# A two-block network in one program: the opening with modulation products on column strips, norms in four steps, and two weight panels multiplied inside the norm loop

## The chip, the cores and the metric

The kernel runs on one core of a Trainium2 chip, as one program. The metric is the device time of one execution in microseconds (us). The change is small against the whole, so the text works in single microseconds.

## What is computed

Two blocks follow each other on 512 tokens of width 1024. The first is a hybrid layer with 256 context tokens beside the 512; the second (attention, a delta rule and two gated feed-forward networks) isn't touched. The part around the change is the head of the hybrid layer:

```
mod   = silu(c) @ ada_w + ada_b                      # 6 * 1024 columns
mod_c = silu(c_ctx) @ ada_w + ada_b
sh1, sc1, g1, sh2, sc2, g2 = split(mod, 6)           # the same for mod_c
h  = rms_norm(x,   norm1_w) * (1 + sc1)  + sh1       # 512 tokens
hc = rms_norm(ctx, norm1_w) * (1 + sc1c) + sh1c      # 256 tokens
p  = h @ w_in                                        # q, k, v, z, xbc, dt
```

All products are in fp32 to the eye of the reference. The kernel makes a large product from three: operand and weights are each split in a high and a low part of type fp32r.

## The kernel before

**Layout.** Features lie on the partitions, in 8 chunks of 128, and tokens along the free dimension. `hh` and `hl` hold the high and the low part of the normed input: for each chunk 512 columns of x and 256 of the context.

**One plan for all engines.** `put` appends a step to a single list. At the end each engine walks through that list and issues, in that order, what the step means for it. So each engine's order is fixed when the program is built, and a step that waits on an engine holds all later steps on that engine. A semaphore wait on TensorE therefore also holds the products of other steps behind it. SyncE issues the loads, in the same order.

**Panels.** A weight panel is 1024 x 128 (512 KB). `load` brings it to one of three buffers `raw0` to `raw2` in turn, `cut` makes its high part on ScalarE (L612) and its low part on VectorE or GpSimd (L622), and `product` multiplies it, chunk by chunk, three products a chunk (high by high, high by low, low by high; L644). Two pairs of split buffers take turns: panel j+2 can be cut only when panel j's products are done. The panels come in the order q (4, on x alone), k and v (4 each, on x and context), dt, xbc, z and so on. Between panels the stream of loads also carries 32 parts of the modulation (`mod`) that are needed late: GpSimd makes them from a panel of `ada_w`, and TensorE and VectorE finish them (`modset`).

**The opening.** `turn_x` turns x and the context to the feature layout: TensorE transposes, ScalarE squares with a sum (L795) and copies (L800). `roots` and `spread` make the reciprocal root of the mean square and spread it over the partitions (L527, L488, L540). Then 16 panels of `ada_w` give scale and shift of the 8 chunks, two panels for each chunk. For panel i, `ada_mm` multiplies (L768) with the two columns silu(c), silu(c_ctx) as weights, 8 products that accumulate in two rows; ScalarE copies the two rows out (L813); `ada_set` transposes them (L776) and VectorE adds the bias (L831). After each second panel `norm1` handles one chunk: VectorE makes the gain (L836) and the scaled x (L846), ScalarE the high part (L819), VectorE the low part (L850), and the same three for the context. All 16 panels and 8 chunks come ahead of the first cut. The load of the second weight panel waits for the last `ada_set`, since `raw2` holds the copied rows until then.

```
for i in range(16):
    if i < 15:
        put("ada_mm", i + 1, banks=1, of=8)
    put("ada_set", i, banks=1, of=8)
    if i % 2:
        put("norm1", i // 2)
```

**A loop that exists already.** `gemm` has a form with `feed`, used later in the program: it calls `feed(c)`, puts the products of the first panel with chunk c, and then those of the second panel with chunk c - 2 (`LAG` is 2), and the third panel is cut after the last chunk.

## Time and profile before

| what | value |
|---|---|
| median of three runs | 2761.59 us (2761.25 to 2764.94) |
| the profiled execution | 2769.39 us, its span 2767.6 us |
| mean granted TensorE clock in it | 0.962 |
| TensorE busy | 2574.6 us, 93% of the span |
| VectorE, ScalarE, GpSimd busy | 50%, 35%, 36% |
| mean DMA rate | 73 GB/s |

The profiled execution has its own time, some 8 us over the median. Differences worked out from its rows are carried over to the median. Starts are in us from the beginning of the span. Neighbouring instructions of one engine overlap in the trace by some tens of nanoseconds, so costs are read from start to start where that can be done. An fp32 product or transpose shows as two records, an fp32r product as one. "PEclk" is the granted clock of TensorE: 1.00 is 2.4 GHz and 0.50 is 1.2 GHz.

### The profile page before, as it was taken

The numbers are of one execution on the slowest core, as the hardware profiler recorded it, in microseconds if no ns is written. First come the engines' busy times: TensorE is split into PE (matmuls) and PEld (weight loads), VectorE is DVE, ScalarE is ACT, GpSimd is POOL, SyncE is SP. The second block draws the span as 40 slices with busy tenths as digits, with TensorE's granted clock in tenths as the row PEclk, the third lists the DMA queues.
The fourth block names the chain that finished last, engine by engine and source line by source line (L and its number), as shares of the span: only waits on it lengthen the run. The fifth ranks groups of instructions, "written<-read, shape, count | busy, mean of one in ns | idle before, by whom it ended". The sixth has DMA issues, their size and how long they took to land.

```text
span 2767.6 us, 45664 instructions
## 1 busy us (share of the span) xinstructions
PE 2574.6 (93%) x19756; PEld 2307.6 (83%) x19756; DVE 1382.0 (50%) x2118; ACT 969.6 (35%) x1525; POOL 986.8 (36%) x585
## 2 busy tenths in 40 slices
PE   6999977899999999999999999999999989999997
PEld 4777766768888787887989999988988978999997
DVE  3545548363535354444175364466654534726363
ACT  4233442332323443333343332354333233333232
POOL 0653334634444422222534444500002214444444
PEclk8999988999999999999999999999998998999998
DMA  7532220323333221111222333322111012233321
GB/s 197 140 110 63 61 78 1 100 75 92 97 93 89 72 62 33 52 39 47 69 62 84 92 89 87 85 66 62 40 40 32 21 32 58 79 90 88 89 86 60
DMA packets 379929, 201.34 MB, mean 73 GB/s; under 512 B 6465, under 2 KB 377153, under 8 KB 379729
## 3 DMA queue, kind: packets, MB, share of 16 engines
q1 hardware_dynamic: 379728, 198.42, 25.5%
q8 instruction: 156, 2.56, 0.4%
q14 instruction: 45, 0.36, 0.0%
HBM read 196.30 MB, written 2.10 MB: 72 GB/s over the span
## 4 chain that ended last, share of the span: by engine, by line
PE 58%; DVE 22%; ACT 10%; issue 5%; POOL 3%; DMA 1%; SPq 0%; POOLq 0%; ACTq 0%; DVEq 0%
PE ps L644 41%; DVE t_ffy L2781 7%; ACT t_wh L612 4%; DVE t_ffy L2784 2%; ACT t_ffy L2688 2%; DVE t_atq L2580 2%; POOL t_wl L622 1%; PE ps L2388 1%; DVE t_ffy L2790 1%; PE ps L3013 1%; DVE t_wl L622 1%; PE ps L2361 1%; PE ps L2327 1%; PE ps L3032 1%; PE ps L1042 1%
## 5 line engine op out<-in xcount | busy, mean ns | idle before, releaser
L622 POOL TENSOR_TENSOR t_wl<-t_raw,t_wh 128x1024 fp32r<-128x1024 f32 (+2 forms) x268 | 610.9, 2280 | 1035.0 <-ACT t_wh L612 1035.0
L612 ACT ACTIVATE t_wh<-t_raw 128x1024 fp32r<-128x1024 f32 (+2 forms) x323 | 327.8, 1015 | 602.4 <-PE ps L644 571.6
L644 PE MATMUL ps<-t_hh,t_wh 128*128 128x264 f32 (+2 forms) x2048 | 474.0, 310 | 15.9 <-ACT t_wh L612 7.7
L644 PE MATMUL ps<-t_hh,t_wl 128*128 128x264 f32 (+2 forms) x2048 | 450.4, 299 | 5.9 <-POOL t_wl L622 5.3
L644 PE MATMUL ps<-t_hl,t_wh 128*128 128x264 f32 (+2 forms) x2048 | 447.5, 300 | 0.0
L644 PEld LDWEIGHTS ps<-t_hh,t_wh 128*128 128x128 f32 x2048 | 324.9, 193 | 38.0 <-issue 16.6
L644 PEld LDWEIGHTS ps<-t_hh,t_wl 128*128 128x128 f32 x2048 | 325.7, 192 | 21.1 <-POOL t_wl L622 6.3
L644 PEld LDWEIGHTS ps<-t_hl,t_wh 128*128 128x128 f32 x2048 | 324.1, 192 | 9.4 <-issue 1.5
L644 PE MATMUL ps<-t_fhh,t_wh 128*128 128x264 f32 (+1 forms) x1040 | 281.9, 325 | 7.6 <-DVE t_fhl L1705 5.6
L644 PE MATMUL ps<-t_fhh,t_wl 128*128 128x264 f32 (+1 forms) x1040 | 280.6, 324 | 4.3 <-POOL t_wl L622 4.2
L2781 DVE SCALAR_TENSOR_TENSOR t_ffy<-t_ffp,t_vec,t_ffy 128x528 f32<-128x528 f32 x88 | 216.4, 2459 | 130.6 <-ACT t_ffy L2688 130.6
L644 PE MATMUL ps<-t_fhl,t_wh 128*128 128x264 f32 (+1 forms) x1040 | 278.3, 323 | 0.0
L644 PEld LDWEIGHTS ps<-t_fhh,t_wh 128*128 128x128 f32 x1040 | 173.8, 190 | 26.8 <-DVE t_fhl L1705 8.2
L644 PEld LDWEIGHTS ps<-t_fhh,t_wl 128*128 128x128 f32 x1040 | 174.1, 190 | 21.6 <-POOL t_wl L622 5.6
L644 PEld LDWEIGHTS ps<-t_fhl,t_wh 128*128 128x128 f32 x1040 | 173.7, 189 | 16.7 <-issue 0.4
L644 PE MATMUL ps<-t_ffh,t_wl 128*128 128x264 f32 x704 | 144.8, 287 | 8.7 <-POOL t_wl L622 7.8
L644 PE MATMUL ps<-t_ffh,t_wh 128*128 128x264 f32 x704 | 144.7, 287 | 5.3 <-ACT t_wh L612 1.5
L644 PE MATMUL ps<-t_ffl,t_wh 128*128 128x264 f32 x704 | 143.4, 285 | 0.0
L2514 DVE TENSOR_TENSOR t_ffp<-ps,t_rstd 128x264 f32<-128x264 f32 x176 | 67.4, 424 | 112.8 <-PE ps L644 111.5
L622 DVE TENSOR_TENSOR t_wl<-t_raw,t_wh 128x1024 fp32r<-128x1024 f32 x55 | 78.4, 1427 | 84.6 <-ACT t_wh L612 84.6
L644 PEld LDWEIGHTS ps<-t_ffh,t_wl 128*128 128x128 f32 x704 | 109.5, 189 | 12.0 <-POOL t_wl L622 12.0
L644 PEld LDWEIGHTS ps<-t_ffh,t_wh 128*128 128x128 f32 x704 | 109.2, 190 | 6.9 <-ACT t_wh L612 5.0
(555 smaller groups left out, 4407.6 us busy)
## 6 DMA issues: line engine op xcount, KB each, us to landing
t_raw<-in_up SPq DMA_DIRECT2D x44, 512.0 KB, 3.9
t_raw<-in_up2a SPq DMA_DIRECT2D x44, 512.0 KB, 3.9
t_raw<-in_up2b SPq DMA_DIRECT2D x44, 512.0 KB, 3.8
t_raw<-in_attn_in SPq DMA_DIRECT2D x33, 512.0 KB, 4.1
t_raw<-in_dn_in SPq DMA_DIRECT2D x33, 512.0 KB, 4.2
t_raw<-in_ada_w SPq DMA_DIRECT2D x32, 512.0 KB, 4.6
t_raw<-in_w_in SPq DMA_DIRECT2D x25, 512.0 KB, 4.2
t_raw<-in_down SPq DMA_DIRECT2D x16, 512.0 KB, 3.8
```

The costliest lines, as they stand in the source:

```text
L612: ac.activation(wh[slot_of[j]][:, 0:kc, :], raw[r % NRAW][:, 0:kc, :], ACT.Copy).then_inc(up("wh_cut", "cut", j), 1)
L622: eng.tensor_tensor(wl[slot_of[j]][:, 0:kc, :], raw[r % NRAW][:, 0:kc, :], wh[slot_of[j]][:, 0:kc, :].bitcast(F), SUB).then_inc(up(name, " ...
L644: ins = pe.matmul(ps[bank_of(j, i)][:, 0:tn], wt[slot][:, k, :], a[:, k, t0:t0 + tn], start=first, stop=last)
L1042: ins = pe.matmul(ps[b][:, 0:64], pts[i % 2][:, 128 * k:128 * k + 128], V[:, v, 64 * h:64 * h + 64], start=k == 0, stop=k == 3)
L2327: pe.matmul(ps[b][0:tn, 0:wide], aq[p % 3][64 * e:64 * e + 64, t0:t0 + tn], ak[p % 3][64 * e:64 * e + 64, a:a + wide], start=True, stop=False)
L2361: pe.matmul(ps[b][0:tn, 0:wide], ak[p % 3][64 * e:64 * e + 64, t0:t0 + tn], aq[p % 3][64 * e:64 * e + 64, q0:q0 + wide], start=True, stop= ...
L2388: ins = pe.matmul(ps[b][64 * e:64 * e + 64, lo - q0:lo - q0 + n], lhs, pT[e][0:tn, P_AT[k] + lo - t0:P_AT[k] + lo - t0 + n], start=k == 0, ...
L2514: ins = dv.tensor_tensor(a[part_, t0:t0 + tn], ap[part_, :], rstd[part_, t0:t0 + tn], MUL)
L2580: dv.reciprocal(tq[m][:, :], tq[m][:, :]).then_inc(up("inverted", "pair_norm", p, m), 1)
L2688: ac.activation(y, fp[par][:, 0:L], ACT.Copy, scale=col(f"f{n}c0", f + NF * par)).then_inc(up("copied", kind, n, f), 1)
L2781: dv.scalar_tensor_tensor(out=y, in0=u[:, 1:1 + L], scalar=col(f"f{n}c1", f + NF * par), in1=y, op0=MUL, op1=ADD).then_inc(st.up(), 1)
L2784: dv.scalar_tensor_tensor(out=y, in0=u[:, 2:2 + L], scalar=col(f"f{n}c2", f + NF * par), in1=y, op0=MUL, op1=ADD).then_inc(up("conved", ki ...
```

## The change

1. `ada_mm` puts its 8 products on four column strips of 32 (k modulo 4 picks the strip); its weights are 32 columns wide (`cs32`, two of them filled, the others zero), and its result has 128 rows. `ada_set` becomes a product of these 128 rows with `add4`, which adds the four strips and turns in one.
2. `norm1` is taken apart into four steps a chunk: scaled x, scaled context (`norm1`), low x, low context (`low1`). The low part of the context of chunk c is put into the turn of chunk c + 1.
3. The products of q's first two panels go into the norm loop: `gemm` gets `feed_first`. In the turn of chunk c come two `ada_mm` and two `ada_set` of the next chunk, the norm steps of c, panel 0 with chunk c, and panel 1 with chunk c - 2.
4. Loads 0 and 1 are now both weight panels and are issued straight behind the first three panels of `ada_w`, and the cuts of both come before the loop. The other `ada_w` loads follow in `ada_rest`. The `mod` parts start with the third panel, and dt gets two.
5. `silu_c` moves to the front; both `roots`, `ada_mm` 0 and 1 and `ada_set` 0 are put ahead of the `spread` steps; the table load for `rope` is put into the first turn.

```diff
--- before.py
+++ after.py
@@ -195,9 +195,10 @@
...
-                if ada_at and stage in ("q", "k", "v", "dt", "xbc", "z", "wo"):
-                    stream.append(("mod", 32 - len(ada_at)))
-                    ada_at.pop(0)
+                for _ in range(2 if stage == "dt" else 1):
+                    if ada_at and len(panels) > 2 and stage in ("q", "k", "v", "dt", "xbc", "z", "wo"):
+                        stream.append(("mod", 32 - len(ada_at)))
+                        ada_at.pop(0)
...
@@ -685,7 +686,10 @@
...
-        row2 = [rows_of(raw[2])[0:2, 128 * i:128 * i + 128] for i in range(2)]
+        spare = rows_of(raw[2])
+        rows2 = [spare[:, 128 * i:128 * i + 128] for i in range(2)]
+        cs32 = spare[:, 256:512].rearrange("p (c j) -> p c j", j=32)
+        add4 = spare[:, 512:514]
...
+            "begin": "scaled/z scaled/s", "norm1": "normed hi_set", "low1": "lo_dve",
...
         put("begin")
+        put("silu_c")
         for i in range(7):
             put("turn_x", i, banks=2, of=8)
             if i < 6:
                 sig.mark("squared", "turn_x", i)
-        put("silu_c")
+        load_to(1)
+        put("ada_rest")
         put_roots(NORM_X)
+        put_roots(NORM_C)
+        put("ada_mm", 0, banks=1)
+        put("ada_mm", 1, banks=1)
+        put("ada_set", 0, banks=1)
         put_spread(NORM_X)
-        put_roots(NORM_C)
         put_spread(NORM_C)
-        put("ada_mm", 0, banks=1, of=8)
-        for i in range(16):
-            if i < 15:
-                put("ada_mm", i + 1, banks=1, of=8)
-            put("ada_set", i, banks=1, of=8)
-            if i % 2:
-                put("norm1", i // 2)
-                take_sqb(("lo_dve", "norm1", i // 2, "x"), "norm1", i // 2, "x")
-                take_sqb(("lo_dve", "norm1", i // 2, "c"), "norm1", i // 2, "c")
+
+        def norm1_of(c, x):
+            put("norm1", c, x)
+            take_sqb(("lo_dve", "low1", c, x), "norm1", c, x)
+
+        def feed_first(c):
+            if c is None:
+                return
+            if c == 0:
+                put("rope_tables")
+            if c < KD:
+                for i in (2 * c + 2, 2 * c + 3):
+                    if i < 16:
+                        put("ada_mm", i, banks=1)
+                    put("ada_set", i - 1, banks=1)
+                    if i == 16:
+                        break
+                norm1_of(c, "x")
+            if 0 < c <= KD:
+                put("low1", c - 1, "c")
+            if c < KD:
+                norm1_of(c, "c")
+                put("low1", c, "x")
 
         def ready_h(p, k):
-            return [("lo_dve", "norm1", k, "c" if len(p.spans) == 2 else "x")]
+            return [("lo_dve", "low1", k, x) for x in "xc"[:len(p.spans)]]
...
-                for i in range(7):
+                for i in range(3):
                     ada_panel(i)
...
-            def turn_x(i):
-                w.wait_ge(s.copied, at("copied", "turn_x", i, "1"))
-                ada_panel(7 + i)
+            def ada_rest():
+                for i in range(3, 7):
+                    ada_panel(i)
+                for i in range(7):
+                    w.wait_ge(s.copied, at("copied", "turn_x", i, "1"))
+                    ada_panel(7 + i)
...
-                    ins = pe.matmul(ps[b][0:2, 0:128], cs[:, k, :], x[:, k, :], start=k == 0, stop=k == KD - 1)
+                    ins = pe.matmul(ps[b][32 * (k % 4):32 * (k % 4) + 32, 0:128], cs32[:, k, :], x[:, k, :], start=k < 4,
+                                    stop=k >= 4)
...
-                pe.transpose(ps[b][:, 0:2], row2[i % 2], C("ident", 2, 2)).then_inc(up("turned", "ada_set", i), 1)
+                w.wait_ge(s.scaled, at("scaled", "begin", "s"))
+                pe.matmul(ps[b][:, 0:2], rows2[i % 2], add4, start=True,
+                          stop=True).then_inc(up("turned", "ada_set", i), 1)
...
+                w.wait_ge(s.scaled, at("scaled", "begin", "z"))
+                ac.activation(cs32[:, :, 0], col("c", 0, 8), ACT.Silu)
+                ac.activation(cs32[:, :, 1], col("c_ctx", 0, 8), ACT.Silu).then_inc(up("cs_ready", "silu_c"), 1)
...
-                ac.activation(row2[i % 2], ps[b][0:2, 0:128], ACT.Copy).then_inc(up("copied", "ada_mm", i), 1)
-
-            def norm1(c):
-                for x, a in (("x", (0, S, 0)), ("c", (S, S + CT, 1))):
...
+                ac.activation(rows2[i % 2], ps[b][:, 0:128], ACT.Copy).then_inc(up("copied", "ada_mm", i), 1)
+
+            def norm1(c, x):
+                a, n, g = (0, S, 0) if x == "x" else (S, CT, 1)
+                i, _ = sqb_at["norm1", c, x]
+                w.wait_ge(s.normed, at("normed", "norm1", c, x))
...
             def begin():
                 dv.memset(eps[:, :], EPS).then_inc(s.eps_set, 1)
+                dv.memset(cs32[:, :, :], 0.0).then_inc(up("scaled", "begin", "z"), 1)
+                w.wait_ge(s.cst_in, 16)
+                dv.tensor_reduce(add4, C("ident").rearrange("p (g h) -> p h g", h=32)[:, 0:2, :], AX.X,
+                                 ADD).then_inc(up("scaled", "begin", "s"), 1)
...
-            def norm1(c):
-                w.wait_ge(s.mod_set, at("mod_set", "ada_set", 2 * c + 1))
-                dv.tensor_scalar(gain1[:, 0:2, c], mod[:, SC1 + c, :], 1.0, col("norm1_w", c), ADD,
...
+            def norm1(c, x):
+                a, n, g, src = (0, S, 0, xl[c]) if x == "x" else (S, CT, 1, ctxT[:, c, :])
+                i, last = sqb_at["norm1", c, x]
+                if x == "x":
+                    w.wait_ge(s.mod_set, at("mod_set", "ada_set", 2 * c + 1))
+                    dv.tensor_scalar(gain1[:, 0:2, c], mod[:, SC1 + c, :], 1.0, col("norm1_w", c), ADD,
+                                     MUL).then_inc(st.up(), 1)
...
+                w.wait_ge(s.rstd_a, at("rstd_a", "spread", NORM_X if x == "x" else NORM_C))
+                if last:
+                    w.wait_ge(handles[last[0]], at(*last))
+                dv.scalar_tensor_tensor(out=sqb[i][:, 0:n], in0=src, scalar=gain1[:, g, c:c + 1], in1=rstd[:, a:a + n],
+                                        op0=MUL, op1=MUL).then_inc(up("normed", "norm1", c, x), 1)
...
+            def low1(c, x):
+                a, n, g = (0, S, 0) if x == "x" else (S, CT, 1)
+                i, _ = sqb_at["norm1", c, x]
+                w.wait_ge(s.hi_set, at("hi_set", "norm1", c, x))
+                dv.scalar_tensor_tensor(out=hl[:, c, a:a + n], in0=sqb[i][:, 0:n], scalar=mod[:, c, g:g + 1],
+                                        in1=hh[:, c, a:a + n].bitcast(F), op0=ADD,
+                                        op1=SUB).then_inc(up("lo_dve", "low1", c, x), 1)
...
-        load_to(NRAW - 1)
-        put("rope_tables")
-        gemm(("q",), then_first)
+        gemm(("q",), then_first, feed=feed_first)
```

## Rows read from the trace of the kernel before

**Rows 1.** The page, part 1: busy time and share of the span by engine.
```profile
PE 2574.6 (93%) x19756; PEld 2307.6 (83%) x19756; DVE 1382.0 (50%) x2118; ACT 969.6 (35%) x1525; POOL 986.8 (36%) x585
```

**Rows 2.** Windows: stretch, length, busy us (count) by engine, PEclk, DMA share, GB/s.
```profile
20.00:33.00 13.00, 8.01 (x37) 5.66 (x38) 0.34 (x2) 5.02 (x12) 0.00 (x0) 0.52 1.19 290
33.00:53.00 20.00, 18.97 (x162) 13.19 (x159) 12.16 (x25) 5.74 (x15) 4.73 (x4) 1.00 0.77 189
...
70.00:74.00 4.00, 0.00 (x0) 0.00 (x0) 2.45 (x5) 1.90 (x3) 0.00 (x0) 0.50 0.84 258
74.00:80.00 6.00, 5.63 (x12) 3.97 (x13) 2.36 (x2) 1.33 (x2) 0.27 (x1) 0.50 0.59 163
```

**Rows 3.** Timeline of the first chunk: start, us, engine, line, what [idle before].
```profile
35.85 0.22 PE L776 MATMUL ps<-t_cst,t_raw 2*128 2x2 f32 x1
...
36.11 0.22 DVE L831 TENSOR_SCALAR t_mod<-ps,t_vec 128x2 f32<-128x2 f32 x1 [1.77 <-PE ps L776]
36.36 0.23 DVE L836 TENSOR_SCALAR t_gain<-t_mod,t_vec 128x2 f32<-128x2 f32 x1
36.62 0.75 DVE L846 SCALAR_TENSOR_TENSOR t_sqb<-t_xT,t_gain,t_rstd 128x512 f32<-128x512 f32 x1
...
37.41 0.72 ACT L819 ACTIVATE t_hh<-t_sqb,t_mod 128x512 fp32r<-128x512 f32 x1 [1.19 <-DVE t_sqb L846]
...
38.17 0.75 DVE L850 SCALAR_TENSOR_TENSOR t_hl<-t_sqb,t_mod,t_hh 128x512 fp32r<-128x512 f32 x1 [0.79 <-ACT t_hh L819]
```

**Rows 4.** Timeline, TensorE: cuts of the first panels and the first products.
```profile
73.24 2.15 ACT L612 ACTIVATE t_wh<-t_raw 128x1024 fp32r<-128x1024 f32 x2
...
74.31 2.36 DVE L622 TENSOR_TENSOR t_wl<-t_raw,t_wh 128x1024 fp32r<-128x1024 f32 x2 [0.46 <-ACT t_wh L612]
...
74.33 0.79 PE L644 MATMUL ps<-t_hh,t_wh 128*128 128x512 f32 x1 [4.87 <-ACT t_wh L612]
...
74.92 0.63 PE L644 MATMUL ps<-t_hl,t_wh 128*128 128x512 f32 x1
...
88.31 0.39 PE L644 MATMUL ps<-t_hh,t_wh 128*128 128x512 f32 x1
88.54 0.39 PE L644 MATMUL ps<-t_hl,t_wh 128*128 128x512 f32 x1
```

**Rows 5.** Timeline of the opening: ScalarE's tables and roots, TensorE's spreads.
```profile
20.44 1.28 ACT L805 ACT_TABLE_LOAD   x1
...
23.36 0.30 ACT L527 ACTIVATE t_roots<-t_ssq,t_eps 128x4 f32<-128x4 f32 x1
...
23.92 2.07 PE L488 MATMUL ps<-t_cst,t_roots 128*128 128x128 f32 x8 [7.79 <-DVE t_roots L560]
```

**Rows 6.** Timeline, TensorE: two panels of the modulation, at either clock.
```profile
28.21 3.57 PE L768 MATMUL ps<-t_vT,t_small 128*2 128x128 f32 x16
...
34.01 1.91 PE L768 MATMUL ps<-t_xbc,t_small 128*2 128x128 f32 x16
```

**Rows 7.** Timeline, TensorE: a sum on column strips (L2724), later in the program.
```profile
948.50 0.42 PE L2724 MATMUL ps<-t_atq,t_cst 128*32 128x264 f32 x2
...
949.21 0.39 PE L2724 MATMUL ps<-t_sqb,t_cst 128*32 128x264 f32 x2
...
949.53 0.39 PE L644 MATMUL ps<-t_hh,t_wh 128*128 128x264 f32 x1
```

**Rows 8.** Timeline, TensorE: one fp32 product with 128 weight columns among others.
```profile
166.56 0.28 PE L783 MATMUL ps<-t_cst,t_part 128*128 128x1 f32 x2
```

**Rows 9.** Windows, TensorE alone: short pauses between bursts, in the scan stage.
```profile
443.00:446.00 3.00, 1.03 (x12) 1.00 0.00 0
...
457.00:459.00 2.00, 0.15 (x2) 1.00 0.00 0
459.00:463.00 4.00, 4.00 (x33) 0.57 0.01 4
```

**Rows 10.** The page, part 6: loads of weight panels: count, size, us to landing.
```profile
t_raw<-in_w_in SPq DMA_DIRECT2D x25, 512.0 KB, 4.2
```

More of the change, by code:

```diff
@@ L745, in ada_mm @@
                     ada_panel(14 + i)
-            return {"begin": begin, "turn_x": turn_x, "ada_mm": ada_mm}
+            return {"begin": begin, "ada_rest": ada_rest, "ada_mm": ada_mm}
         def front_tensor(pe, w, held, free):
@@ L858, in modset @@
                                  ADD).then_inc(up("mod_set", "modset", n), 1)
-            return {"begin": begin, "ada_set": ada_set, "norm1": norm1, "modset": modset}
+            return {"begin": begin, "ada_set": ada_set, "norm1": norm1, "low1": low1, "modset": modset}
         def front_gpsimd(po, w, st):
```

26 lines of the change are left out of this document (4 added, 22 removed).

## The prediction

> **What bounds the kernel now.** I read the page first: TensorE is busy for 93% of the span [rows 1], so over most of the program only TensorE's work and its waits count. The windows show where that doesn't hold, and the reader is to see that the change sits there: TensorE idles four microseconds just before the first product at 74.33, and the clock is at its lower level then and for six microseconds of products after it [rows 2]. The timeline of one chunk shows what the opening waits on: a chain of VectorE and ScalarE steps that pass one tile to and fro [rows 3]. TensorE is nearly full beside it from 33 to 53, but with the small products of the modulation [rows 2, 6]. The DMA engines run at 290 GB/s to 33 and at 189 in the mean of 33 to 53 [rows 2]; 3.8 MB at 290 take 13 us, so they are dry from about 46, and the loads don't set the pace there. From 80 on TensorE is full. What the change is worth is therefore the start of panel q2, the first product that neither version mixes into the norms: 88.31 before, since q0 and q1 take from 74.33 up to there [rows 4]. Any shift of it is carried to the end, because the order behind it is unchanged and TensorE-bound.
>
> **What the change removes and moves.** Removed: 16 panels of `ada_mm` at 1.91 us each at the full clock or 3.57 at the lower [rows 6], and the stretch 74.33 to 88.31 as a stretch of its own. Added: strips, a wider `ada_set`, and above all a new order on TensorE. The product of q0 with chunk c waits for the low part of x of that chunk, and in TensorE's list the `ada_mm` and `ada_set` that VectorE needs for chunk c+1 stand behind it. VectorE's next step in turn waits for them. So the loop becomes a ring: products, modulation, norm chain, products, with little of it beside anything else. Before, the norm chain and the modulation ran side by side.
>
> **When the loop begins.** ScalarE's copies end at 20.44. One table load goes (silu is done early, while ScalarE waits for x), so the first root starts at 21.7, two roots of 0.3 us end at 22.3, then two copies of rows (0.27 each). TensorE does `ada_set` 0 (0.5 at the lower clock) and both spreads, 2.07 us and half as much, together 3.1 [rows 5], and ends at 26.1. ScalarE's copy of the context's root ends at 26.5, the two cuts take 2.15 [rows 4] to 28.6. VectorE's two low parts take 2.36 [rows 4] to 30.0. Then bias and gain, scaled x, high and low part as in [rows 3]: from bias start to the end of the low part 36.11 to 38.92, and a second bias: the low part of chunk 0 is done at 33.0. Panels of `ada_w`, 512 KB each, come at 290 GB/s [rows 2], 1.8 us each, behind the two weight panels: the fourth by about 25 and the last by about 46, ahead of each turn. The lower bound here is 31 (cuts beside the spreads' end), the upper 35 (weight panels late); I take 33.
>
> **One turn of the ring**, from the low part of chunk c to that of c+1. First number the full clock, second the lower:
> - q0 with chunk c, three products of 512 columns: 0.23 each at the full clock (88.31 to 88.54), 0.43 at the lower, the first after a wait 0.59 (74.33 to 74.92) [rows 4]: 0.80, 1.45.
> - q1 with chunk c-2: 0.68, 1.28.
> - two `ada_mm`. No row has this form. The nearest is the sum on four strips: 16 records of 264 columns from 948.50 to the next product at 949.53, so 1.03 us; with 128 columns 0.48 to 0.50, and at the lower clock 0.9 [rows 7]. The other bound is no gain from strips, 1.91 and 3.57 [rows 6]. I take the strips, since they are the same form in the same program: 0.96, 1.80.
> - the first `ada_set`, now two records with 128 weight columns, 0.28 by [rows 8]: 0.25, 0.40.
> - four changes between whole array and strips: the last strip record starts at 949.21 and the next product at 949.53, where 0.22 is a strip's pace: 0.1 each [rows 7]: 0.40, 0.45.
> - the second `ada_set` until VectorE starts, 0.26 before for two weight rows [rows 3], with wide weights 0.35, 0.55.
> - bias 0.25, gain 0.26, scaled x 0.79, high part 0.76, low part 0.80 [rows 3]: 2.86 at either clock. The context's steps hide in the wait for ScalarE; uncovered they would cost about 0.8, half of x's two VectorE steps, the context being half as wide.
>
> That is 6.30 or 8.79 us. Two of the seven turns lack q1 (5.62, 7.51), the last lacks the `ada_mm` (4.89, 6.36). Sum: 41.3 or 56.5. Behind it stand q0's last chunk and three of q1: 2.8 or 5.3. q2 needs its load, which waits for the last `ada_set` and takes 4.2 us [rows 10], then a cut of 1.06: that is 5.3 after `ada_set` 15, while q1 ends 6 to 9 us after it, so q1 hides it; without that cover it would cost up to 1 us. The load of q3 and of the first `mod` part, and the rope tables, are queued behind that load on SyncE; with 1.5 MB at 290 GB/s they land about 5 us later, under q2. Two `mod` parts at dt are 9.5 us of GpSimd (4.73 for one, the four instructions of 33 to 53 [rows 2]) beside dt and two panels of 24 products each on 768 columns, at 0.34 us (0.23 for 512) 8 us a panel, so they cost nothing; if one of the next loads waited for them, it would be up to 1 us.
>
> The Trainium skill (TensorEngine Tiling, Key Properties) says that a change of the tiling mode drains TensorE, which speaks against switching four times a turn; the rows of the strips agree, with 0.1 us a change. Without that rule the sum would be some 2.5 us less. The skill (TensorE: Matmul & The Clock Gate, Part 3) gives a measured 2.38 times for three column strips; by that a block would take 0.80 at the full clock and the twelve blocks of the turns 4 us more.
>
> **The clock decides.** q2 starts at 33.0 + 41.3 + 2.8 = 77.1 if the clock is full all through, at 33.0 + 56.5 + 5.3 = 94.8 if it is low. In between it is 77.1 + 17.7 s for a share s at the lower level; 88.31 is met at s = 0.63. Each turn leaves TensorE idle for 3.2 us. In the scan stage a pause of 2 us brings the lower level for over three microseconds in one place (457 to 463) and not in another (443 to 446) [rows 9], and in the opening six microseconds of products passed before the level rose [rows 2]. The loop also starts at the lower level, after the idle time at 17 to 33. A burst at the lower level is 5.5 us long, so the clock should rise near its end, when the pause comes. I take s = 0.8: 77.1 + 14.2 = 91.3. That is 3.0 us later than before. From the median: 2761.6 + 3.0 = 2764.6 us. (The span of the profiled execution would go from 2767.6 to 2770.6; its own time is 8 us above the median, and the difference is carried over.)
>
> **The rivals.**
> - *The clock stays at its full level.* Bursts and pauses are as dense as in the stretch at 443 that kept it [rows 9]. Against it: the pause here is longer than 2 us in every turn, and the loop starts low. q2 at 77.1, 11.2 us early: 2750.4, faster. It decides from s below 0.32, where the gain passes 5.5 us.
> - *The clock stays low throughout.* The bursts hold strips and small products, and q2's first products would still be slow. q2 at 94.8 and up to 1 us for the rise: 2768 to 2769, slower. It decides from s above 0.94, or from 0.4 us more a turn than I count.
> - *The strips don't run side by side.* Fourteen blocks stay at 3.57 in place of 0.9, 2.7 us each: 37 us, so about 2800. The rows of the strips speak against it [rows 7].
> - *The ring isn't closed*, because VectorE's or ScalarE's steps overlap more than I see, or the changes and the wide `ada_set` are hidden: up to 1 us a turn less, 2757.
>
> **How the numbers follow.** A measurement of this kernel tells about 0.2%, or 5.5 us, from no change. I give the forecast (s about 0.6 to 0.94) 0.48, the full clock or most of it 0.22, the low clock throughout or longer turns 0.24, the open ring 0.05 (half of it inside 5.5 us), serial strips 0.01. So faster 0.27, same 0.48, slower 0.25. The time is that of the likeliest, 2764.6; its own range is 2759 to 2768. The range for 8 times in 10 takes in the full clock on one side and the low one on the other: 2749 to 2771.
>
> **What the profile after would show.** `ada_mm` blocks of 16 records in 0.5 or 0.9 us; two cuts before 30; the first product of q0 near 33; a turn of 6 to 9 us with a pause of 3.2 on TensorE between `ada_set` and the next product, released by VectorE's low part; PEclk mostly 0.50 from 20 to about 90; q2's first product at 91; no new wait between there and dt. The prediction is wrong if the clock holds in the loop, if the turn is longer for a reason I haven't listed (a load of `ada_w` that is late behind the two weight panels, a bank), or if the stretch behind q2 isn't full and gives the shift back.

## The result, and the profile after

| | median us | runs | ratio to before |
|---|---|---|---|
| before | 2761.3 | 6 (2760.5 to 2764.9) | |
| after | 2780.5 | 6 (2774.7 to 2788.2) | 1.0069 (1.0050 to 1.0088) |

The change costs 19 us (0.7%), where 3 were forecast and the range ended at 2771. A second set of runs on another chip gave 2782.2 against 2766.2, ratio 1.0056 (1.0039 to 1.0073). The profiled execution took 2777.8 us, its span 2776.0, so the two spans differ by only 8.4: the profiled execution of before lies 8 us over its median, that of after 3 under it. Lines of the new kernel are shifted: the product is L645, `ada_mm` L794, `ada_set` L804, VectorE's low part L888, `modset` L812 and L895.

Windows of after (columns as in [rows 2]):

```profile
20.00:33.00 13.00, 6.24 (x51) 5.30 (x52) 5.22 (x11) 7.08 (x16) 0.00 (x0) 0.67 1.14 286
33.00:53.00 20.00, 14.25 (x120) 9.14 (x119) 6.05 (x16) 4.13 (x10) 0.00 (x0) 0.53 0.80 193
53.00:70.00 17.00, 11.31 (x84) 7.61 (x84) 5.81 (x16) 3.57 (x8) 0.00 (x0) 0.60 0.00 0
70.00:80.00 10.00, 4.72 (x42) 3.19 (x42) 5.26 (x13) 3.02 (x6) 0.00 (x0) 0.78 0.01 2
80.00:90.00 10.00, 6.89 (x18) 5.51 (x19) 3.77 (x8) 2.78 (x4) 0.81 (x1) 0.54 0.61 155
90.00:100.00 10.00, 10.00 (x43) 7.89 (x42) 7.55 (x6) 1.66 (x3) 9.61 (x7) 1.00 0.65 189
```

From 33 to 53 TensorE was full at the full clock before [rows 2]; now it is busy for 14.25 of 20 us at PEclk 0.53. The timeline of the first turn and of the ring's end:

```profile
26.35 1.99 ACT L613 ACTIVATE t_wh<-t_raw 128x1024 fp32r<-128x1024 f32 x2
...
29.97 0.22 DVE L874 TENSOR_SCALAR t_gain<-t_mod,t_vec 128x2 f32<-128x2 f32 x1
30.23 0.75 DVE L881 SCALAR_TENSOR_TENSOR t_sqb<-t_xT,t_gain,t_rstd 128x512 f32<-128x512 f32 x1
...
31.77 0.75 DVE L888 SCALAR_TENSOR_TENSOR t_hl<-t_sqb,t_mod,t_hh 128x512 fp32r<-128x512 f32 x1 [0.39 <-ACT t_hh L850]
...
32.66 0.76 PE L645 MATMUL ps<-t_hh,t_wh 128*128 128x512 f32 x1 [3.65 <-DVE t_hl L888]
...
34.21 1.08 PE L794 MATMUL ps<-t_xbc,t_raw 128*32 128x128 f32 x16
...
35.23 0.59 PE L804 MATMUL ps<-t_raw 128*128 128x2 f32 x2
...
40.16 0.79 PE L645 MATMUL ps<-t_hh,t_wh 128*128 128x512 f32 x1 [2.81 <-DVE t_hl L888]
...
55.69 0.80 PE L645 MATMUL ps<-t_hh,t_wh 128*128 128x512 f32 x1 [2.81 <-DVE t_hl L888]
...
64.50 0.79 PE L645 MATMUL ps<-t_hh,t_wh 128*128 128x512 f32 x1 [2.81 <-DVE t_hl L888]
...
86.26 0.79 PE L645 MATMUL ps<-t_hh,t_wh 128*128 128x512 f32 x1 [2.94 <-DVE t_hl L888]
...
90.49 0.40 PE L645 MATMUL ps<-t_hh,t_wh 128*128 128x512 f32 x1
```

The rows with "<-DVE t_hl L888" are the starts of q0's product with a chunk. The first is at 32.66, the last at 86.26: seven turns in 53.6 us. A turn at the low clock is 64.50 - 55.69 = 8.8. Each ends in a pause of 2.8 us. q2 starts at 90.49, against 88.31 before [rows 4]. So the opening went as forecast and cost 2.2 us. The stretch behind it did not:

```profile
175.32 1.91 POOL L904 TENSOR_TENSOR t_raw<-t_raw,t_small 128x1024 f32<-128x1024 f32 x1
...
177.00 0.72 PE L812 MATMUL ps<-t_cst,t_part 128*128 128x1 f32 x6
...
180.32 0.45 POOL L913 TENSOR_TENSOR t_part<-t_raw 128x128 f32<-128x128 f32 x1
...
180.92 0.35 PE L812 MATMUL ps<-t_cst,t_part 128*128 128x1 f32 x2 [3.19 <-POOL t_part L913]
...
557.02 0.46 POOL L913 TENSOR_TENSOR t_part<-t_raw 128x128 f32<-128x128 f32 x1
...
563.84 0.20 DVE L895 TENSOR_SCALAR t_mod<-ps,t_vec 128x1 f32<-128x1 f32 x1
...
564.06 1.84 PE L476 MATMUL ps<-t_cst,t_rstd 128*128 128x1 f32 x8 [4.25 <-DVE t_mod L895]
```

GpSimd begins the second of dt's two `mod` parts at 175.32 and ends it at 180.77. TensorE is through with v's last panel at 177.00, does three `modset` products and waits 3.19 us for the fourth; behind it the clock falls (0.57 from 181 to 184, where before has 1.00):

```profile
180.00:190.00 10.00, 9.08 (x43) 7.89 (x44) 0.22 (x1) 0.00 (x0) 5.02 (x6) 0.83 0.59 157
```

At 564.06 the norm behind wo waits 4.25 us. The same place in before waits 0.61, and its eight products take 1.02 us in place of 1.84. The row of after names the last `modset` (L895), but that step is only 0.2 us at the end of a chain. Rows around it in after, then in before; the first row is wo's last product and the last row the first of up1:

```profile
556.32 0.39 PE L645 MATMUL ps<-t_mh,t_wl 128*128 128x512 f32 x1
...
557.49 2.37 POOL L623 TENSOR_TENSOR t_wl<-t_raw,t_wh 128x1024 fp32r<-128x1024 f32 x1
559.80 1.27 POOL L553 TENSOR_TENSOR t_rstd<-t_rstd,t_sqb 128x512 f32<-128x512 f32 x1
...
561.17 2.74 DVE L553 TENSOR_TENSOR t_rstd<-t_rstd,t_sqb 128x512 f32<-128x512 f32 x1 [3.43 <-POOL t_rstd L553]
...
571.88 0.59 PE L645 MATMUL ps<-t_fhh,t_wh 128*128 128x512 f32 x1
```
```profile
545.21 1.28 POOL L552 TENSOR_TENSOR t_rstd<-t_rstd,t_sqb 128x512 f32<-128x512 f32 x1
546.33 0.39 PE L644 MATMUL ps<-t_mh,t_wl 128*128 128x512 f32 x1
...
548.45 0.69 DVE L552 TENSOR_TENSOR t_rstd<-t_rstd,t_sqb 128x512 f32<-128x512 f32 x1 [0.69 <-ACT t_sqb L514]
...
549.29 1.02 PE L475 MATMUL ps<-t_cst,t_rstd 128*128 128x1 f32 x8 [0.61 <-DVE t_rstd L552]
...
555.14 0.47 PE L644 MATMUL ps<-t_fhh,t_wh 128*128 128x512 f32 x1 [0.52 <-DVE t_fhl L1705]
```

GpSimd works on the late part until 557.48 and only then on a low cut (L623) and on its share of the norm's sum of squares (L553). VectorE's share waits 3.43 us for that and then takes 2.74 us in place of 0.69, with GpSimd's next low cut beside it (561.02 to 563.37). wo's last panel starts 10.0 us later than in before (551.02 against 541.00), so TensorE would have started this norm at 559.3; of the 4.75 us more, 2.7 are the late start of VectorE's share and 2.05 its length. With the slower products behind it, from wo's last product to up1's first it takes 15.6 us in place of 8.8 (556.32 to 571.88, 546.33 to 555.14): 6.7 more. The other profiles agree: 15.1 to 15.6 us where the parts are one panel late there (after, e4, e5, e13), 19.0 and 20.2 where they are two late (e9, e1), 8.6 to 8.8 in the other eight. The 2.74 stands in all six profiles of kernels whose parts are late there (after, e1, e4, e5, e9, e13), 0.69 in the other eight.

**Where the time goes, by cuts.** ScalarE's cuts come in the same order in both kernels, so the start of the n-th cut is a common mark. After minus before:

| cut | what | before | after | difference |
|---|---|---|---|---|
| 8th | k3 | 119.61 | 121.36 | +1.8 |
| 14th | first of xbc | 175.52 | 177.26 | +1.7 |
| 15th | behind dt's `mod` parts | 184.66 | 191.48 | +6.8 |
| 27th | ahead of the scan stage | 386.08 | 394.82 | +8.7 |
| 34th | up1, behind the scan stage and wo | 541.42 | 556.35 | +14.9 |
| 36th | up1, behind the norm | 571.56 | 588.20 | +16.6 |

Nothing happens between the eighth and the fourteenth, 5.1 us are lost at dt, 1.9 up to the 27th, 6.2 in the scan stage and wo, 1.8 around the norm behind wo. The 34th cut isn't a mark of TensorE's progress, though: in after it waits 4.8 us for its load, and TensorE's last product of wo is 10.0 us later than in before, not 14.9. On TensorE the differences are 2.2 at q2, 6.8 behind dt (where it turns the rows of dt, 193.57 against 186.75), 10.0 at the end of wo and 16.7 at up1's first product. From there on both kernels issue the same work; it takes 2196.0 us at a mean clock of 0.969 in the profile of before and 2187.8 at 0.976 in that of after.

### The profile page after: what moved, and what is told of

Its sections match the earlier page's. It is cut to its first block, busy times and chain, and to the rows that moved or that the text cites. A ratio compares the mean times of both kernels' runs of the same rounds, so it can differ in the third digit from the quotient of the medians.

```text
span 2776.0 us, 45700 instructions
## 1 busy us (share of the span) xinstructions
PE 2564.5 (92%) x19772; PEld 2298.8 (83%) x19772; DVE 1384.4 (50%) x2120; ACT 969.4 (35%) x1525; POOL 990.0 (36%) x585
## 4 chain that ended last, share of the span: by engine, by line
PE 57%; DVE 22%; ACT 10%; issue 5%; POOL 4%; DMA 1%; POOLq 0%; ACTq 0%; SPq 0%; DVEq 0%
PE ps L645 41%; DVE t_ffy L2817 7%; ACT t_wh L613 4%; DVE t_ffy L2820 2%; ACT t_ffy L2724 2%; DVE t_atq L2616 2%; POOL t_wl L623 1%; PE ps L2424 1%; DVE t_wl L623 1%; DVE t_ffy L2826 1%; PE ps L3049 1%; PE ps L2397 1%; PE ps L2363 1%; PE ps L1078 1%; PE ps L3068 1%
## 5 line engine op out<-in xcount | busy, mean ns | idle before, releaser
L623 POOL TENSOR_TENSOR t_wl<-t_raw,t_wh 128x1024 fp32r<-128x1024 f32 (+2 forms) x268 | 611.5, 2283 | 1029.9 <-ACT t_wh L613 1029.9
L645 PE MATMUL ps<-t_hh,t_wh 128*128 128x264 f32 (+2 forms) x2048 | 477.4, 312 | 35.7 <-DVE t_hl L888 23.5
L645 PE MATMUL ps<-t_hh,t_wl 128*128 128x264 f32 (+2 forms) x2048 | 452.5, 300 | 6.3 <-POOL t_wl L623 4.3
L645 PE MATMUL ps<-t_hl,t_wh 128*128 128x264 f32 (+2 forms) x2048 | 449.1, 301 | 0.0
L645 PEld LDWEIGHTS ps<-t_hh,t_wh 128*128 128x128 f32 x2048 | 325.5, 193 | 58.3 <-issue 21.3
L645 PEld LDWEIGHTS ps<-t_hh,t_wl 128*128 128x128 f32 x2048 | 325.8, 192 | 22.8 <-POOL t_wl L623 6.8
L645 PEld LDWEIGHTS ps<-t_hl,t_wh 128*128 128x128 f32 x2048 | 324.6, 192 | 9.4 <-issue 1.5
L645 PE MATMUL ps<-t_fhh,t_wh 128*128 128x264 f32 (+1 forms) x1040 | 280.4, 323 | 6.6 <-DVE t_fhl L1741 4.9
L645 PE MATMUL ps<-t_fhh,t_wl 128*128 128x264 f32 (+1 forms) x1040 | 281.5, 324 | 4.1 <-POOL t_wl L623 3.7
L645 PE MATMUL ps<-t_fhl,t_wh 128*128 128x264 f32 (+1 forms) x1040 | 278.4, 323 | 0.0
L645 PEld LDWEIGHTS ps<-t_fhh,t_wh 128*128 128x128 f32 x1040 | 173.3, 189 | 25.9 <-DVE t_fhl L1741 7.9
L645 PEld LDWEIGHTS ps<-t_fhh,t_wl 128*128 128x128 f32 x1040 | 173.8, 189 | 21.9 <-POOL t_wl L623 6.6
L645 PEld LDWEIGHTS ps<-t_fhl,t_wh 128*128 128x128 f32 x1040 | 173.4, 189 | 17.2 <-issue 0.4
L645 PE MATMUL ps<-t_ffh,t_wl 128*128 128x264 f32 x704 | 145.4, 288 | 8.5 <-POOL t_wl L623 7.8
L645 PE MATMUL ps<-t_ffh,t_wh 128*128 128x264 f32 x704 | 145.2, 287 | 5.2 <-ACT t_wh L613 1.5
L645 PE MATMUL ps<-t_ffl,t_wh 128*128 128x264 f32 x704 | 144.2, 287 | 0.0
L645 PEld LDWEIGHTS ps<-t_ffh,t_wl 128*128 128x128 f32 x704 | 110.4, 191 | 11.8 <-POOL t_wl L623 11.8
L623 DVE TENSOR_TENSOR t_wl<-t_raw,t_wh 128x1024 fp32r<-128x1024 f32 x55 | 77.5, 1412 | 85.0 <-ACT t_wh L613 85.0
L645 PEld LDWEIGHTS ps<-t_ffh,t_wh 128*128 128x128 f32 x704 | 109.9, 191 | 6.9 <-ACT t_wh L613 5.0
```

What stands on the lines that cost most here:

```text
L623: eng.tensor_tensor(wl[slot_of[j]][:, 0:kc, :], raw[r % NRAW][:, 0:kc, :], wh[slot_of[j]][:, 0:kc, :].bitcast(F), SUB).then_inc(up(name, " ...
L645: ins = pe.matmul(ps[bank_of(j, i)][:, 0:tn], wt[slot][:, k, :], a[:, k, t0:t0 + tn], start=first, stop=last)
```

## The experiments

Twelve kernels, in three sets of runs, each set on one chip with the kernel before in it. "Difference" is the median minus that of the kernel before in the same set (2762.7 with e1 to e4, 2761.6 with e5 to e9, 2766.2 with e10 to e13). The last column is the start of the 36th cut in the profiled execution, minus 571.56.

| kernel | median | difference | ratio, 95% | 36th cut |
|---|---|---|---|---|
| e1_mod_late | 2777.6 | +14.9 | 1.0026 to 1.0054 | +14.1 |
| e2_dt_double | 2767.9 | +5.2 | 0.9996 to 1.0017 | +0.5 |
| e3_late_start | 2770.2 | +7.4 | 1.0008 to 1.0033 | +3.7 |
| e4_ring_open | 2752.8 | -9.9 | 0.9943 to 0.9974 | -15.2 |
| e5_busy_pause | 2765.3 | +3.6 | 1.0003 to 1.0020 | +5.9 |
| e7_mods_early | 2766.9 | +5.3 | 1.0004 to 1.0026 | +7.4 |
| e8_ring_open_mods_early | 2741.8 | -19.8 | 0.9912 to 0.9941 | -18.8 |
| e9_before_mods_late | 2767.8 | +6.1 | 1.0008 to 1.0031 | +6.6 |
| e10_strips_alone | 2763.1 | -3.1 | 0.9982 to 1.0001 | -1.4 |
| e11_busy_and_mods_early | 2755.3 | -11.0 | 0.9939 to 0.9971 | -10.6 |
| e12_shift_two | 2767.7 | +1.5 | 0.9995 to 1.0014 | +4.8 |
| e13_changed_again | 2782.2 | +16.0 | 1.0039 to 1.0073 | +14.8 |

The differences are worth some 3 us either way: single runs of the kernel before range from 2759 to 2775, and the profiled execution is only one of them. Where median and ratio disagree, as in e1 (14.9 against 0.40%, or 11 us) and e2 (5.2 against 0.07%, or 2 us), the ratio with its interval is the safer figure.

### The `mod` parts

**e1_mod_late**: the changed kernel with one part at dt; the part left over comes at wo's last panel.

```diff
-                for _ in range(2 if stage == "dt" else 1):
+                for _ in range(2 if stage == "wo" and m == 7 else 1):
```

> The changed kernel, but with the 32nd mod part moved: dt carries one again and the last panel of wo two. The traces show that before dt's product all modset steps are flushed, and that TensorE waits there 3.2 us for a part that GpSimd hasn't finished, after which the clock is at its lower level for 3 us. Theory A (that wait and what the clock adds is a cost of its own): 5 us less than the changed kernel, about 2775 where that one gives 2780, and q's and dt's stretch in the trace as long as before. Theory B (the loss is the norm loop's and what a later start does to the rest, the wait at dt only moves idle time): within 1 us of the changed kernel. Theory C (the later stages lose and gain by the clock alone, by where in its rhythm they start): no telling, anything from 2763 to 2785, with a spread of several us between runs.

The wait at dt is gone (from the 14th to the 15th cut it takes 9.2 us in place of 14.2), and yet the time is only 1 to 4 us under that of the changed kernel (+14.9 against +19.2 and, again, +16.0). That lies between its first two theories, 5 us and within 1. TensorE's timeline of e1 shows where it went:

```profile
551.13 0.35 PE L812 MATMUL ps<-t_cst,t_part 128*128 128x1 f32 x2 [0.80 <-POOL t_part L913]
555.66 0.56 PE L812 MATMUL ps<-t_cst,t_part 128*128 128x1 f32 x2 [4.18 <-POOL t_part L913]
562.04 1.33 PE L476 MATMUL ps<-t_cst,t_rstd 128*128 128x1 f32 x8 [2.46 <-DVE t_mod L895]
```

The parts now stand two panels late up to the end, and three waits in a row stand ahead of the norm (the third is again VectorE's share of the sum, 2.74 us long). That turned the question from dt to the place of all the parts.

**e2_dt_double**: the kernel before, with two parts at dt (the `for` line of the change alone, without the late start).

> The kernel before, with one edit of the change alone: dt carries two mod parts. Nothing of the opening is touched. Theory A: TensorE waits about 3 us ahead of dt's product, and the time is 3 to 5 us above the kernel before, 2765 to 2766. Theory B: no difference, 2761. Theory C: the shift of 3 to 5 us at 180 changes the clock in the stages behind, and the time moves by more than the wait, up to 2775, with a wider spread than the 4 us of the kernel before.

The wait appears without the rest of the change, so this line alone is enough for it:

```profile
178.02 0.56 PE L784 MATMUL ps<-t_cst,t_part 128*128 128x1 f32 x2 [3.18 <-POOL t_part L876]
```

From the 14th to the 15th cut it takes 15.4 us against 9.1, so 6.3 are lost there with the lower clock behind it (0.50 from 181 to 184). The median is 5.2 higher, but the interval runs from -1 to +5 us: that the whole program pays for this wait is likely, and not shown by this kernel alone.

**e9_before_mods_late**: the kernel before, its parts starting at the third panel as in the change, with e1's double part at wo's last panel.

```diff
-                if ada_at and stage in ("q", "k", "v", "dt", "xbc", "z", "wo"):
-                    stream.append(("mod", 32 - len(ada_at)))
-                    ada_at.pop(0)
+                for _ in range(2 if stage == "wo" and m == 7 else 1):
+                    if ada_at and len(panels) > 2 and stage in ("q", "k", "v", "dt", "xbc", "z", "wo"):
+                        stream.append(("mod", 32 - len(ada_at)))
+                        ada_at.pop(0)
```

> The kernel before with one edit: the mod parts start with the third panel, as in the change, dt has one, and wo's last panel two, so that every part from there on stands two panels later than before. The opening is untouched. Theory D: nothing at dt, but TensorE waits for late modset steps in the wo stage and behind it, and the time is 6 to 12 us above the kernel before, 2768 to 2774. Theory C or a cost of the opening alone: within 2 us of the kernel before.

It is 6.1 us slower, and that is the price of late parts less a gain. In before, GpSimd makes the first part from 47.77 to 52.73, in the middle of the opening's norm loop, and VectorE's steps beside it are longer; these two take 0.48 and 0.75 elsewhere in the loop:

```profile
48.49 1.47 DVE L850 SCALAR_TENSOR_TENSOR t_hl<-t_sqb,t_mod,t_hh 128x256 fp32r<-128x256 f32 x1 [0.57 <-ACT t_hh L819]
...
51.14 1.29 DVE L846 SCALAR_TENSOR_TENSOR t_sqb<-t_xT,t_gain,t_rstd 128x512 f32<-128x512 f32 x1
```

Two turns (44.59 to 49.88 and on to 55.34) take 5.3 and 5.5 us in place of 4.3, and a later one (59.64 to 65.17) takes 5.5, behind products of TensorE at a lower clock (0.65 from 57 to 61). In e9 no part stands there and every turn takes 4.2 to 4.3: the first cut starts at 69.27, against 72.5 to 73.2 in the four profiles that have the old opening whole (before, e2, e3, e12), and q2 at 83.76, against 88.31 in before and 87.17 in e2. So 3.4 to 4.6 us are won in the opening, and the late parts lose about 10 (6.1 and that gain). The trace has the loss in one place: from wo's last product to up1's first it takes 19.0 us against 8.8, 10.2 more.

**e7_mods_early**: the changed kernel, with the two parts made up at k's second and v's first panel.

```diff
-                for _ in range(2 if stage == "dt" else 1):
+                for _ in range(2 if (stage, m) in (("k", 1), ("v", 0)) else 1):
```

> The changed kernel with its two postponed mod parts made up for in k1 and v0 (two parts each), dt with one: from v1 on every part stands where it stood before the change. Theory D (the part at dt and the later parts in the wo and scan stage each cost: TensorE waits 3.2 us at dt, and 4.2 us for a modset step, with a longer GpSimd queue, at 560 to 590; the clock falls behind each): 10 to 15 us less than the changed kernel, 2766 to 2770, so 4 to 7 us above the kernel before, of which 2 to 3 are the opening. Theory C (what follows the opening is the luck of the clock): less than 4 us below the changed kernel.

Of the 19 us 14 are gone: 5.3 over before are left, as its first theory had it (4 to 7). Neither wait is there: the 14th to 15th cut takes 9.2 us, the 34th to 36th 30.1, and the norm behind wo waits as it did before:

```profile
556.64 1.02 PE L476 MATMUL ps<-t_cst,t_rstd 128*128 128x1 f32 x8 [0.61 <-DVE t_rstd L553]
```

GpSimd has room there for a second part: beside k and v TensorE stands idle for 0.1 us in all from q2 to the end of v.

### The pause and the clock

**e5_busy_pause**: the changed kernel, with three small products on constants in the pause of each turn.

```diff
                 norm1_of(c, "x")
+                put_busy("front", c, 3)
```

> The changed kernel with three extra products of ones by the constants (256 columns, results unused) on TensorE in each turn of the norm loop, in the pause between the second ada_set and the next product of q0. Theory A (the clock is low in the loop because each turn has a pause of 2.8 us): the extra products take 1.3 us of that pause at the full clock or 2.6 at the lower, the clock rises in the first or second turn and stays, a turn falls from 7.5 to 8.8 us to about 6.2, q2 starts 8 to 12 us sooner than the 90.5 of the changed kernel, and the time falls by as much. Theory B (small products and strips keep the clock low whatever stands in the pause): turns as before or longer by the extra products, no gain.

Windows and timeline of e5:

```profile
33.00:53.00 20.00, 15.76 (x179) 10.78 (x177) 8.84 (x22) 5.65 (x14) 0.00 (x0) 1.00 0.76 191
53.00:70.00 17.00, 12.76 (x110) 9.12 (x111) 8.39 (x20) 5.06 (x11) 0.00 (x0) 1.00 0.01 1
```
```profile
56.04 0.50 PE L645 MATMUL ps<-t_hh,t_wh 128*128 128x512 f32 x1 [1.41 <-DVE t_hl L889]
...
57.30 0.40 PE L645 MATMUL ps<-t_hh,t_wl 128*128 128x512 f32 x1
57.63 0.64 PE L795 MATMUL ps<-t_vT,t_raw 128*32 128x128 f32 x16
58.20 0.38 PE L805 MATMUL ps<-t_raw 128*128 128x2 f32 x2
...
59.34 1.54 PE L498 MATMUL ps<-t_cst 128*128 128x256 f32 x6
...
62.29 0.50 PE L645 MATMUL ps<-t_hh,t_wh 128*128 128x512 f32 x1 [1.41 <-DVE t_hl L889]
```

With 1.54 us of products of no use in a pause of 2.95 the clock is full all through, and a turn takes 62.29 - 56.04 = 6.25 us in place of 7.5 to 8.8. q2 starts at 76.12, 14.4 us earlier than in the changed kernel, more than the 8 to 12 of the first theory. The median is 12 to 16 us under that of the changed kernel (+3.6 against +19.2 and +16.0).

**e4_ring_open**: the changed kernel, with the modulation and norm steps of chunk c + 1 put ahead of the products with chunk c.

```diff
-        def feed_first(c):
-            if c is None:
-                return
-            if c == 0:
-                put("rope_tables")
+        def norm_steps(c):
             if c < KD:
...
+        def feed_first(c):
+            if c == 0:
+                put("rope_tables")
+                norm_steps(0)
+            if c is not None and c < KD:
+                norm_steps(c + 1)
```

> The changed kernel with the norm loop put one chunk ahead: the modulation and the norm steps of chunk c+1 stand before the products of chunk c in every engine's order, so VectorE and ScalarE work on c+1 while TensorE multiplies c. The two mod parts at dt stay. Theory A (the loop is a ring in which TensorE and the norm chain wait for one another in turn): a turn falls from 7.5 to 8.8 us to about 5, q2 starts 15 to 20 us sooner, at 71 to 75, and the time is 13 to 20 us below the changed kernel. Theory B (the turn is bound by TensorE's work at the lower clock and by the loads): less than 5 us below it.

TensorE's timeline of e4:

```profile
43.45 0.48 PE L645 MATMUL ps<-t_hh,t_wh 128*128 128x512 f32 x1
...
46.54 0.35 PE L807 MATMUL ps<-t_raw 128*128 128x2 f32 x2
46.75 0.48 PE L645 MATMUL ps<-t_hh,t_wh 128*128 128x512 f32 x1
...
53.01 0.50 PE L645 MATMUL ps<-t_hh,t_wh 128*128 128x512 f32 x1 [1.21 <-DVE t_hl L891]
```

The products with one chunk now cover VectorE's work on the next: a turn in the middle takes 46.75 - 43.45 = 3.3 us with no pause, at PEclk 0.92 from 33 to 53; the last two have pauses of 1.2 and 1.1. The eighth cut starts at 91.5, 30 us earlier than in the changed kernel. That is more than the first theory had (a turn of 5 us, 13 to 20 us in all; it is 26 to 29). The waits for the `mod` parts are still there (3.2 us at dt's place, 4.2 behind wo); with them the program is only 10 us faster than before, where its eighth cut is 28 us earlier, and without them 20 (e8).

**e11_busy_and_mods_early**: e5 and e7 together.

> The changed kernel with both cures together: three small extra products in each pause of the loop, and the two double mod parts at k's second and v's first panel in place of dt. Theory A (the clock in the loop and the place of the mod parts are two separate causes): the gains add, 15 and 13.6 below the changed kernel's 2780.5, so about 2752, and no wait on mod parts from dt to wo. Theory B (both mostly move the same later clock phases about): the sum is well short of that, 2760 to 2766.

Against the kernel before in the same set of runs, the four combinations are:

| | pause empty | products in the pause |
|---|---|---|
| `mod` parts as in the change | +19.2, again +16.0 | +3.6 |
| `mod` parts made up early | +5.3 | -11.0 |

Down each column the difference is 11 to 15 us, along each row 12 to 16: two separate causes, and their prices add within the spread of the medians. The first theory's sum was 9.6 under a kernel before of 2761.6; measured are 11.0 under one of 2766.2.

**e8_ring_open_mods_early**: e4 and e7 together, the fastest of the kernels.

> The norm loop one chunk ahead (as the run with the ring open) and the mod parts made up for in k1 and v0. Theory D: the gains add up; the run with the ring open gave 2752.8, less 10 to 14 is 2739 to 2743. Theory C: within 4 us of 2753.

It beats both kernels: 19.8 us under before (ratio 0.9926, 0.9912 to 0.9941) and 39 under the changed kernel. The parts are worth 10 us here (e4 to e8). Filling the pause wasn't tried in this loop, which has hardly a pause; its clock is 0.72 from 33 to 53 all the same.

### The shift by itself

**e3_late_start**: the kernel before, with five extra copies (5.4 us) ahead of ScalarE's first cut. **e12_shift_two**: the same with two (2.1 us).

```diff
+                for n in range(5 if j == 0 else 0):
+                    ac.activation(wh[0][:, :, :], raw[0][:, :, :], ACT.Copy).then_inc(s.late, 1)
+                    w.wait_ge(s.late, n + 1)
```

> The kernel before, with a pure delay: five more copies of the first panel's high part on ScalarE, one after another, ahead of the first product, so that everything from there on is 5.5 us later and nothing else is changed. Theory A or B (a shift is carried to the end as it is): 5 to 6 us above the kernel before, 2767, with a spread like that of the kernel before. Theory C (where the stages start decides when TensorE's clock falls and rises in the attention, scan and delta stages): more than 8 us above or less than 3, and the stretches of 386 to 572 and 1875 to 2350 change in length by several us each.

> The kernel before with ScalarE's first cut delayed by two extra copies of 1.06 us each, so that all that follows starts 2.2 us later, as in the changed kernel, and in the old order. Theory A (a shift costs about itself, up to a third more by the clock of later stages): 2763.5 to 2765. Theory B (even a small shift upsets the later stages): 2768 or more, and then the opening alone explains a good part of the loss.

```profile
79.06 0.80 PE L647 MATMUL ps<-t_hh,t_wh 128*128 128x512 f32 x1 [10.32 <-ACT t_wh L615]
```
```profile
75.74 0.79 PE L647 MATMUL ps<-t_hh,t_wh 128*128 128x512 f32 x1 [7.06 <-ACT t_wh L615]
```

These are the first product of e3 and of e12: 4.7 and 1.4 us later than at 74.33 [rows 4] (5.3 and 2.0 later than in e2, which has the same opening), so e12's shift is about that of the changed kernel or a little less. The medians are 7.4 and 1.5 higher. So a shift costs about itself and perhaps some 3 us more, which these spreads can't tell from nothing; it doesn't grow into 19. The second theory of e12, that a small shift upsets the later stages, falls.

### The strips alone, and the changed kernel again

**e10_strips_alone**: the kernel before with the column strips and the wide `ada_set` (part 1 of the change), order as before.

```diff
-                    ins = pe.matmul(ps[b][0:2, 0:128], cs[:, k, :], x[:, k, :], start=k == 0, stop=k == KD - 1)
+                    ins = pe.matmul(ps[b][32 * (k % 4):32 * (k % 4) + 32, 0:128], cs32[:, k, :], x[:, k, :], start=k < 4,
+                                    stop=k >= 4)
...
-                pe.transpose(ps[b][:, 0:2], row2[i % 2], C("ident", 2, 2)).then_inc(up("turned", "ada_set", i), 1)
+                pe.matmul(ps[b][:, 0:2], rows2[i % 2], add4, start=True,
+                          stop=True).then_inc(up("turned", "ada_set", i), 1)
```

> The kernel before with the column strips of ada_mm and the wide ada_set alone; order of all steps, loads and cuts as before. Theory A (the strips take TensorE's work, but VectorE and ScalarE set a turn of the old loop: in the trace of before a turn takes 4.4 us from bias to bias, of which TensorE stands in the chain only with the turning product): only the two blocks ahead of the first chunk get shorter, 3.57 and 2.35 down to 1.0 each, and the last set is a little longer. The first product comes 3 to 4 us earlier, 2757 to 2759 in the median. Theory B (TensorE's blocks set the turn): 14 blocks of 1.27 us less, first product 15 us earlier, 2745. Theory C (with less work TensorE's clock stays low in the loop and behind it): no gain, 2760 to 2765.

Windows and timeline of e10:

```profile
33.00:53.00 20.00, 10.17 (x124) 7.26 (x120) 13.35 (x26) 6.27 (x16) 4.99 (x4) 0.53 0.75 186
53.00:70.00 17.00, 8.14 (x92) 5.74 (x84) 11.10 (x26) 5.26 (x12) 0.00 (x0) 0.50 0.13 34
```
```profile
71.54 0.79 PE L644 MATMUL ps<-t_hh,t_wh 128*128 128x512 f32 x1 [4.79 <-ACT t_wh L612]
```

TensorE's busy time from 33 to 53 falls from 18.97 [rows 2] to 10.17 us, and the first product comes 2.8 us earlier, not 15: in the old loop VectorE and ScalarE set the turn, as the first theory said. The clock is at its lower level, as the third had it, and takes part of the gain back: the chunks start 4.4 us earlier (the gain's bias at 31.71, before at 36.11), but a turn takes 4.6 to 4.7 us in place of 4.3, and 7.3 beside GpSimd's part. The median is 3.1 us lower, and the interval takes in 1: a gain isn't shown.

**e13_changed_again**: the changed kernel, on the chip of the runs above it.

> The changed kernel as it is, on the chip of the other three runs of this call, so that they can be compared with it on one chip. Both theories: 2777 to 2782.

## Why the prediction was wrong

**The opening was right, term by term.** The first product of q0 was forecast at 33.0 and came at 32.66. The two cuts ended at 28.3 (26.35 and 1.99), forecast 28.6; from the gain at 29.97 to the product it was 2.7, forecast 2.6. A turn at the low clock: 8.79 forecast, 8.8 measured; at the full clock, which only e5 shows, 6.30 and 6.25. The seven turns: 41.3 + 0.8 x 15.2 = 53.5 forecast, 53.6 measured, which makes the share at the lower level 0.81; the granted clock says the same, 0.60 in the mean from 32.66 to 90.49, so a share of 0.80. That the share was met is in part luck: the text chose 0.8 between two rivals from three places in the trace. From a block of strips to the `ada_set` behind it are 1.02 us at the low clock (34.21 to 35.23), forecast 0.9 and a change of 0.1. The pause was 3.2 forecast, 2.8 to 2.9 measured. q2 at 90.49 against 91.3: the tail was 0.6 us shorter. Its load was hidden by q1. One gain was left out of the list of what is removed: the `mod` part of 47.77 to 52.73 stands in the norm loop of before and not in that of the changed kernel (see e9). The sum was right without it, since its terms come from rows that it doesn't touch and the start of q2 before, 88.31, has it in. The clock was the largest lever in the opening, as the text said: the full clock was to be worth 14.2 us, and e5 shows 14.4 at q2 (76.12, where the sum for the full clock said 77.1) and 12 to 16 in the whole.

The Trainium skill (TensorEngine Tiling, Key Properties) says that a change of the tiling mode drains TensorE. The trace agrees as far as it can, with a small price: in e5 the last product of a turn starts at 57.30, its pace is 0.23, and the strips start at 57.63, so 0.1 us is lost, whether by a drain or by something else. The Trainium skill (TensorE: Matmul & The Clock Gate, Part 3) measured 2.38 times for three column strips, by which a block would take 0.80; here the four strips take 0.57 from start to start (57.63 to 58.20), the change included, against 1.84 before (34.01 to 35.85 [rows 3, 6]).

**The first step that failed** is "Two `mod` parts at dt are 9.5 us of GpSimd ... so they cost nothing; if one of the next loads waited for them, it would be up to 1 us". The sum set GpSimd's 9.5 us against the products of dt and two panels. But TensorE doesn't take the parts after those panels: its `modset` of the second part stands ahead of dt's own products, in a list with a fixed order. So the cover was not 16 us of products but what was left of v's last panel when GpSimd began the second part, 1.7 us (175.32 to 177.00) of its 5.4, and the three small products behind it. It is 3.19 us of wait and 5.1 from cut to cut in the changed kernel; by itself, on the kernel before, 6.3 from cut to cut and 2 to 5 us in the whole, with an interval that takes in zero (e2). The text named the cover, but didn't look up who waits for the parts and where that waiter stands.

**The second is "Any shift of it is carried to the end, because the order behind it is unchanged and TensorE-bound."** The shift is carried to the end (e3, e12; 4.7 us became 7.4, within what medians tell from itself), but the order behind it is changed, so what the sum put at nothing there has a price, the larger of the two. The change starts the `mod` parts at the third panel, two panels late, and makes up only one at dt, so that the last one keeps GpSimd until 557.48, ahead of its low cut and its share of the norm behind wo: 4.25 us of wait on TensorE in place of 0.61, and 6.7 us more from wo's last product to up1's first. The late start of the parts was even listed among the changes, but the text priced only the double part at dt. Late parts alone, on the kernel before, cost 6.1 in the median (e9), and about 10 when the gain in that kernel's opening is taken out; there they are two panels late, not one. Making up both in k and v takes 11 to 15 us away from the changed kernel, with or without products in the pause, and 10 from the open ring.

**The sum put right.** 2761.6 + 2.2 (opening) + 5.1 (dt, from cut to cut) + 6.7 (behind wo) = 2775.6; 2780.5 was measured, and against the kernel before in the same set 16 and 19 us more, where this sum has 14. The two terms for the `mod` parts, 11.8 together, fit the 10 to 15 us that making them up early is worth. With both parts made up early what is left of the change is +5.3 (e7): 2766.9, inside the range and within 3 us of the forecast of +3.0.

**What stays open.** The 2 to 5 us that are missing. In the two profiles 3.2 us are lost on TensorE between dt and the end of wo (6.8 to 10.0), with no wait that answers to them. The stretch from the 27th to the 34th cut goes from 150.9 (e2) to 162.7 (e5) over the profiles, with a clock that is low for 27 to 44 us of it, and one profile of each kernel doesn't settle how much belongs to the parts. e2's profile has won back nearly all it lost at dt by the 36th cut, but that profile is the fastest of its twelve runs. Nor did a run hold GpSimd off VectorE: that the steps of 2.74 and 1.29 us are long because of what GpSimd does beside them is argued from where they stand, not tested.

**The rivals.** The full clock was excluded by the windows (0.53 and 0.60), the low clock throughout as well (0.60 and 0.78 in two of them); the strips do run side by side; the open ring exists only when the order is changed (e4). None of them named the later panels, so the range left out the side on which the result lay. (In the chances, the half of the open ring that was to lie inside 5.5 us belongs to "same" and not to "faster"; nothing hangs on it.)

## What to carry to other kernels

When a step that feeds later work is moved or doubled, follow each of its consumers in the fixed order of every engine up to the last one: cover is what stands ahead of the waiting instruction, not what is busy at the same time. A consumer can be a step of another kind on the engine that makes the part: here GpSimd's own share of a norm stood behind it. Where a loop alternates products and a chain on other engines, put the chain's next inputs ahead of the products with what is ready: here that alone turned 7.5 us a turn into 3.3. A faster product form is worth little where another engine sets the turn, and it can cost the clock.

## What the runs showed of the hardware

- Pauses of 2.8 us in a turn of 7.5 hold TensorE mostly at 1.2 GHz (PEclk 0.53 from 33 to 53). With 1.54 us of products on constants in each pause it is at 2.4 GHz all through (1.00), and the program is 12 to 16 us shorter. The first product of q2 comes 14.4 us earlier, where the expectation had 8 to 12.
- Less work on TensorE lowered the clock: with strips alone it is busy for 10.17 us of 20 at 0.53, before for 18.97 at 1.00. The same 16 records take 1.08 us there and 0.64 in e5, at 1.00.
- VectorE's steps are longer in places where GpSimd works beside them: its add of 128x512 in the norm behind wo takes 2.74 us beside GpSimd's low cut (six profiles) and 0.69 without (eight), and in the opening of before the scaled x takes 1.29 us beside a `mod` part and 0.75 elsewhere.
